# Attention outputs made in columns by pairs of heads, four expert tiles loaded beside the weight ring, and one wait placed later

## The reference, cut to what matters

```python
# part A, layer l
p = sink_softmax(concat([s_loc, s_ctx]), sink)          # 8 heads of 64, 2 key heads
o = p @ v                                               # per head: [128 queries, 64]
o_x = concat([o, local_mixers(...)]) @ w_out[l]
x = layer_norm(ALPHA * x + g1 * o_x, ln1_g[l], ln1_b[l])
y = hier_moe(x * (1 + sc2) + sh2, ...)                  # 2 of 32 experts a token: silu(xb@w1)*(xb@w3) @ w2
# part B, layer l
swa = softmax_with_sink(q_a k_a^T, band) @ v_a          # times a silu gate g_a
fox = softmax(q_b k_b^T + c_i - c_j, causal) @ v_b      # times a silu gate g_b
x += concat([swa, fox, ssm]) @ w_out_2
x += memory_attention(x)
```

## Time and profile before

| what | value |
|---|---|
| median of 3 runs | 2305.1 us (2302.08 to 2305.42) |
| the profiled execution's own time | 2304.22 us |
| its span, first to last instruction | 2302.4 us |
| PE busy | 2035.6 us, 88% of the span |
| mean granted TensorE clock | 0.985 |
| moved by the transfer engines | 640.95 MB, 278 GB/s on average |

### The profile page before, as it was taken

How to read it: one execution, slowest core, us unless ns; L and a number is a source line. 1 busy time by engine, 2 the same in 40 slices (tenths; PEclk the granted TensorE clock), 3 DMA queues, 4 the chain that set the end, 5 groups by cost and what they waited for, 6 DMA issues and landing times.

```text
span 2302.4 us, 30476 instructions
## 1 busy us (share of the span) xinstructions
PE 2035.6 (88%) x11971; PEld 1212.3 (53%) x11972; DVE 786.6 (34%) x1836; ACT 457.2 (20%) x1059; POOL 189.7 (8%) x240
## 2 busy tenths in 40 slices
PE   6999999799877789999877777798999999999998
PEld 4566566444433335757433333344875575775574
DVE  1355674111111116656111111114466312456413
ACT  2142112111111112411111111111123212123112
POOL 1000001111111110001111111111000000000000
PEclk9999999999999999999999999999999999999999
DMA  9235649999999985686999999996343332343230
GB/s 376 110 129 240 255 156 378 423 426 427 427 425 426 425 345 211 236 317 257 424 425 425 424 425 425 427 420 242 134 182 129 111 147 110 147 165 129 95 142 19
DMA packets 62872, 640.95 MB, mean 278 GB/s; under 512 B 15868, under 2 KB 16420, under 8 KB 24240
## 3 DMA queue, kind: packets, MB, share of 16 engines
q1 hardware_dynamic: 41728, 588.39, 61.9%
q0 software_dynamic: 19984, 44.74, 5.5%
q10 hardware_dynamic: 1056, 6.37, 0.7%
HBM read 622.50 MB, written 44.17 MB: 290 GB/s over the span
## 4 chain that ended last, share of the span: by engine, by line
PE 62%; DMA 31%; DVE 4%; ACT 2%; issue 1%; SPq 0%; POOL 0%; DVEq 0%
DMA ring<-in_moe 26%; PE ps L866 10%; PE ps L1037 10%; PE ps L519 8%; PE ps L1051 6%; PE ps L1148 5%; PE ps L507 3%; PE ps L695 3%; DMA ring<-in_denseA 3%; PE ps L1220 2%; PE ps L872 2%; PE ps L1016 2%; PE ps L541 2%; PE ps L771 2%; PE ps L584 1%; DMA ring<-in_denseB 1%
## 5 line engine op out<-in xcount | busy, mean ns | idle before, releaser
L866 PE MATMUL ps<-ring,scr 128*64 128x256 f32 (+1 forms) x4800 | 667.5, 430 | 178.2 <-DMA ring<-in_moe 169.3
L866 PEld LDWEIGHTS ps<-ring,scr 128*64 128x64 f32 x4800 | 333.4, 138 | 485.9 <-DMA ring<-in_moe 239.3
L1833 DVE TENSOR_TENSOR scr<-ps,scr 128x512 f32<-128x512 f32 (+3 forms) x98 | 54.6, 558 | 574.6 <-PE ps L866 487.0
L1037 PE MATMUL ps<-ring,hT 128*128 128x512 f32 (+1 forms) x576 | 245.5, 578 | 5.1 <-ACT hT L1546 5.1
L519 PE MATMUL ps<-ring,hT 128*128 128x512 f32 (+1 forms) x512 | 199.3, 547 | 0.5 <-ACT hT L1516 0.5
L1444 POOL DMA_INDIRECT ys_scratch<-scr,ytab x128 | 125.0, 976 | 825.4 <-DVE scr L2495 791.6
L1670 ACT ACTIVATE scr<-ps 128x512 f32<-128x512 f32 x64 | 38.2, 597 | 760.8 <-PE ps L866 694.0
L2495 DVE COPY scr<-ps 128x1024 f32<-128x1024 f32 x64 | 78.4, 1224 | 269.3 <-PE ps L866 243.4
L1037 PEld LDWEIGHTS ps<-ring,hT 128*128 128x128 f32 x576 | 108.1, 193 | 117.8 <-issue 108.2
L1516 ACT ACTIVATE scr<-ps 128x256 f32<-128x256 f32 (+2 forms) x168 | 71.3, 436 | 403.7 <-PE ps L507 403.7
L519 PEld LDWEIGHTS ps<-ring,hT 128*128 128x128 f32 x512 | 97.3, 193 | 93.0 <-issue 89.2
(11 more groups left out here) (330 smaller groups left out, 2019.2 us busy)
## 6 DMA issues: line engine op xcount, KB each, us to landing
ring<-in_moe SPq DMA_DIRECT2D x192, 2048.0 KB, 15.9
ring<-in_denseB SPq DMA_DIRECT2D x48, 2048.0 KB, 7.7
ring<-in_denseA SPq DMA_DIRECT2D x36, 2048.0 KB, 16.2
scr<-ys_scratch POOLq DMA_DIRECT2D x6, 1024.0 KB, 7.2
modB<-mod_scratch POOLq DMA_DIRECT2D x10, 512.0 KB, 11.3
ring<-kv_scratch SPq DMA_DIRECT2D x2, 2048.0 KB, 8.6
tok_scratch<-hb POOLq DMA_DIRECT2D x6, 512.0 KB, 2.9
memT_scratch<-modB ACTq DMA_DIRECT2D x2, 1024.0 KB, 6.7
```

The lines of the kernel that those rows point to most:

```text
L866: last = mm(out, lhs(c)[:, 0:64], w(c)[:, half * q:half * (q + 1)], start=(c == 0), stop=(c == n - 1))
L1037: last = mm(T["open"][:, 0:cols], hT16[:, c, t * P:(t + 1) * P], w[:, c, 0:cols], start=(c == 0), stop=(c == DC - 1))
L1833: return V.tensor_tensor(out, a, b, op)
```

## The change

- **Attentions in pairs** (the 48 units of part A and 64 of part B; the memory attention keeps its way). The values become the standing operand (64 columns) and the turned weights move (128 columns). The two heads of a pair go to the two column halves of the array, and the result comes out with its columns on the partitions, as `w_out` needs it, so that turning the outputs goes. The weights are now divided by their sum before they are turned, by the DVE (`scaled`), and the PE waits for that (`p_scaled`) and no longer for the exponential. The sink is an extra column of the scores, which takes away the ACT detour. DVE and ACT now go through a pair in the order scores, scores, scale, scale, extras; ACT's side jobs (`serve`) come after both copies of a pair. Some side jobs move one unit later. The gates `ga` and `gb` are made in columns.
- **Tiles beside the ring** (`ASIDE`). Expert tile 3 of layer 0 and expert tiles 3, 7 and 10 of layer 1 get homes of their own in `modB`, `hb`, `S`, `hT` and `scr`, and their transfers are issued before tile 2 of the layer (that of layer 1's tile 3 even before tile 0). The gathers have two buffers in `hb` in place of four for it.
- **The wait on `kv_out`** moves from the end of part A behind the first products of row block 1 in part B.

```diff
+ASIDE = ((3,), (3, 7, 10))
...
-TURNED = ("x0", "x1", "x2", "qb", "kb")
+TURNED = ("x0", "x1", "x2", "qb", "kb", "ga", "gb")
...
+    low_mod, low_rows = (v[:, 2:4, :].rearrange("p a b -> p (a b)") for v in (modB, hb))
+    aside = (((low_mod, low_rows),),
+             ((S[:, 2:4, :].rearrange("p a b -> p (a b)"), low_rows), (low_mod, hT[:, half_tile:2 * half_tile]),
+              (scr[:, 10400:10400 + half_tile], scr[:, 10400 + half_tile:10400 + 2 * half_tile])))
...
+    def in_ring(l, at):
+        return baseM[l] + at - sum(a < at for a in ASIDE[l])
...
+        def paired_attention(units, score, values, nkc, fill):
+            T["p"] += len(units)
+            for i in range(2):
                 score(*units[i])
-            T["bank"] = None
-            def turn_weights(i):
+            fill(0)
+            for i in range(0, len(units), 2):
+                n, h = units[i]
+                for k in (i, i + 1):
+                    need("scaled", p_scaled)
+                    turn_weights(k, nkc(n))
+                    turned = T["tp"]
+                    if k == i:
+                        for at in range(i + 2, min(i + 4, len(units))):
+                            score(*units[at])
+                    if k > 0:
+                        fill(k)
+                if h == 0:
+                    T["bank"] = av_bank()
+                pe.wait_ge(tp_free, turned)
+                for b in range(nkc(n)):
+                    for q in range(2):
+                        last = mm(T["bank"][HD * q:HD * q + HD, h // 2 * P:(h // 2 + 1) * P], values(n, h + q, b),
+                                  sbuf_pT[:, q, b, :], start=(b == 0), stop=(b == nkc(n) - 1))
+                if h == NH - 2:
+                    last.then_inc(av_full, 1)
...
-            attention([(n, h) for n in range(nt) for h in range(NH)],
+            paired_attention([(n, h) for n in range(nt) for h in range(NH)],
                       gqa_score(qTA, kTA, lambda n: 0 if n < NX else 256, lambda n: 512),
                       lambda n, h, k: vA[:, k + (0 if n < NX else 2), (h // GQA) * HD:(h // GQA + 1) * HD],
-                      lambda n: 4 if n < NX else 2, HD, fill)
-            for t in range(nt):
-                need("h", h_ready)
-                turn([hb[:, t, i * P:(i + 1) * P] for i in range(4)])
+                      lambda n: 4 if n < NX else 2, fill)
+            need("h", h_ready, nt)
...
-                    of_rows(mk_at - 2 + j, t, 0, 512)
+                    w = tile(mk_at - 2 + j)
+                    rows_times(lambda c: hb[:, t, c * P:(c + 1) * P] if c < 4 else hT8[:, c, t * P:(t + 1) * P],
+                               lambda c: w[:, c, :], 512)
...
+            def moe_tile(i, at, width):
+                if type(i) is int and at in ASIDE[l]:
+                    n = ASIDE[l].index(at)
+                    pe.wait_ge(aside_in[l][n], 32)
+                    per = half_tile // width
+                    return lambda c: aside[l][n][c // per][:, c % per * width:(c % per + 1) * width]
...
-            for t in range(NX):
-                need("h", h_ready)
-                for c in (0, 4):
-                    turn([mixB[:, t, (c + i) * P:(c + i + 1) * P] for i in range(4)])
+            need("h", h_ready)
+            out_attended(0, 0)
+            need("h", h_ready)
             pe.wait_ge(tp_free, T["tp"])
-            out_attended(0, 0)
...
-            dense(lambda i: d["moe"][l][tile_of(*in_order[i])], 3 * UNROLL - 1, G0)
-            with sp_.Fori(0, E // UNROLL - 1) as i:
+            B0 = blocks_before[l]
+            def load_aside(n):
+                src = d["moe"][l][tile_of(*in_order[ASIDE[l][n]])]
+                for k in range(2):
+                    sp_.dma_start(aside[l][n][k], src[:, k * half_tile:(k + 1) * half_tile]).then_inc(aside_in[l][n], 16)
+            def expert_tile(at):
+                dense(lambda i: d["moe"][l][tile_of(*in_order[at])], 1, in_ring(l, at))
+            if l > 0:
+                sp_.wait_ge(*free_when["turned", l])
+                load_aside(0)
+            expert_tile(0)
+            expert_tile(1)
+            sp_.wait_ge(*free_when["routed", l])
+            sp_.wait_ge(rows_out, (96, 144)[l])
+            if l == 0:
+                sp_.wait_ge(tok_out, 16 * 4)
+                load_aside(0)
+            else:
+                load_aside(1)
+                load_aside(2)
+            for at in range(2, 6 * UNROLL - 1):
+                if at not in ASIDE[l]:
+                    expert_tile(at)
+            with sp_.Fori(1, E // UNROLL - 1) as i:
...
-                if k >= 4:
-                    pool.wait_ge(rows_T, 2 * (K0 + k - 3))
-                pool.indirect_dma_start(hb[:, k % 4, :], None, tok_d,
+                if k >= 2:
+                    pool.wait_ge(rows_T, 2 * (K0 + k - 1))
+                pool.indirect_dma_start(hb[:, k % 2, :], None, tok_d,
...
+        def weights(i, n, h, nk):
+            T["nm"] += 1
+            act.wait_ge(nm_ready, T["nm"])
+            A(sbuf_p[:, i % 2, 0:nk], sbuf_s[:, i % 2, 0:nk], ACT.Exp, bias=nm[:, n, h:h + 1],
+              accum_out=rsum[:, n, h:h + 1]).then_inc(p_ready, 1)
+        def paired_attention(units, nkc, sink, serve, after=None):
+            for i in range(0, len(units), 2):
+                for k in (i, i + 1):
+                    n, h = units[k]
+                    weights(k, n, h, P * nkc(n) + sink)
+                for k in (i, i + 1):
+                    copy_turned(sbuf_pT[:, k % 2, 0:nkc(units[k][0]), :], nkc(units[k][0]))
+                    if after:
+                        after(k)
+                if i > 0:
+                    serve(i - 1)
+                serve(i)
+            serve(len(units) - 1)
...
+        def paired_attention(units, keys, masks, cq, sink, finish, extra, ck=None):
+            def scores(i):
+                n, h = units[i]
+                bank = score_bank()
                 nk = keys(n)
                 s = sbuf_s[:, i % 2, 0:nk]
-                m = masks(n) if masks else None
-                if scale:
-                    tell(ts(s, bank[:, 0:nk], scale(n), None, ALU.mult), sc_free)
-                elif m is None:
+                m = masks(n)
+                if sink:
+                    go(V.tensor_copy(sbuf_s[:, i % 2, nk:nk + 1], snk[:, h:h + 1]))
+                if m is None:
...
+            def scaled(i):
+                n, h = units[i]
+                p = sbuf_p[:, i % 2, 0:keys(n)]
+                dve.wait_ge(p_ready, T["p"] + i + 1)
+                step(V.reciprocal(rinv[:, n, h:h + 1], rsum[:, n, h:h + 1]))
+                tell(ts(p, p, rinv[:, n, h:h + 1], None, ALU.mult), p_scaled)
+            for i in range(0, len(units), 2):
+                for k in (i, i + 1):
+                    scores(k)
+                for k in (i, i + 1):
+                    scaled(k)
+                if i > 0:
+                    extra(i - 1)
+                extra(i)
+                if i > 0 and units[i][1] == 0:
+                    finish(units[i][0] - 1, av_job())
+            extra(len(units) - 1)
+            finish(units[-1][0], av_job())
+            T["p"] += len(units)
...
-                if i == 2:
+                if i == 3:
                     answer()
                     gate_moments((0, 1))
                     root()
-                if i == 4:
+                if i == 5:
                     answer()
                     gate_norm()
...
+            def put_turned(n, bank):
+                tell(V.tensor_copy(hb[:, n, 0:512], bank), av_free)
                 tell(V.tensor_copy(mx[:, 1:2], mx[:, 0:1]), h_ready)
...
-                dve.wait_ge(kv_out, 16 * 2 * DEPTH)
...
                 bank = acc_job()
+                if l == 0 and t == 1:
+                    dve.wait_ge(kv_out, 16 * 2 * DEPTH)
...
-                if i == 12:
+                if i == 13:
```

More of the change, by code:

```diff
@@ new lines, in memory_attention @@
+        def memory_attention(units, score, values, beside):
+            for i in range(2):
+                score(*units[i])
+            for i, (n, h) in enumerate(units):
+                need("p", p_ready)
+                turn_weights(i, 2)
+                turned = T["tp"]
+                if i + 2 < len(units):
+                    score(*units[i + 2])
+                beside(i)
+                pe.wait_ge(tp_free, turned)
+                if h % 2 == 0:
+                    T["bank"] = av_bank()
+                for k in range(2):
+                    last = mm(T["bank"][:, h % 2 * 256:(h % 2 + 1) * 256], sbuf_pT[:, i % 2, k, :], values(h, k),
+                              start=(k == 0), stop=(k == 1))
+                if h % 2 == 1:
+                    last.then_inc(av_full, 1)
@@ L1932, in attention @@
[L1932 to L1939 removed]
+                done()
+                least(n, h, s, sink)
+            def scaled(i):
[4 more added lines that the diff above has]
```

(1 more changed line is left out.)

289 lines of the change are left out of this document (124 added, 165 removed).

## The result

The changed kernel took 2316.8 us (median of 5, 2311.75 to 2318.3) where the kernel before took 2305.1 (median of 5, 2302.08 to 2306.91). The ratio is 1.0048, 95% interval 1.0036 to 1.0061: slower by 0.5%. The forecast was 2280, in a range of 2260 to 2297. The profiled execution took 2318.3, 14.1 more than that of before. Its span is 2316.5 against 2302.4, and the trace splits this difference.

A forecast was written before the change was run, and what follows sets the result against it. It took transfers to bound the expert stretches and TensorE part B's attentions, with part A's mixed. Terms 4.0 - 2.5 + 12 + 0 + 5.1 + 6.0 = 24.6 us gave 2280 us, range 2260 to 2297.

The forecast's parts named there:

- Layer 0's one tile: Layer 0's experts: tile loaded beside the ring, worth at most 4.93 us, against later gathers; taken as 0 (-6 to +3).
- Part B: Both attentions and the unturned outputs in part B: +3.0 us gained per layer (1 to 6), 6.0 for both.
- The sums: Part B's sliding window attention: running sums go out one unit later, back near when needed; priced at 0.8 us a layer.
- The weighing: Multiplying weights with values in two column halves: two records cost what one did, saving 3.0 us per part B attention.
- The forgetting attention: Part B, each layer: VectorE's longer pairs cost 4.9 us against 3.0 saved by weighing; -1.9 us.
- The turns of the outputs: Part B, each layer: attention outputs no longer need turning on TensorE; +3.1 us gained.
- Layer 1's attention: Part A, layer 1: 3.8 us saved before the projection tile's release, less waits and late rows; -2.5 us (-5 to +3).
- Layer 0's attention: Part A, layer 0: 7.6 us saved less 3.6 for first pair, gelu and extras; gain 4 us (1 to 8).
- Layer 1's tiles: Layer 1's experts: three tiles loaded beside the ring into idle transfer time; gain 12 us (8 to 14.8).
- The wait on `kv_out`: Start of part B: the moved wait removes TensorE's idle time; gain 5.1 us (0 to 5.5).
- rival C: Attentions: halves don't overlap or each shape change costs, all weighing savings go; 2304 or 2315 us, chance 0.05.
- Rival B: Layer 0's gathers make TensorE 6 to 8 us late, layer 1's attention gives back 5; 2292 us, chance 0.17.

The follow-up runs named there:

- e6: Changed kernel with layer 0's tile back in the ring, four gather buffers there, and the running sums at unit 12: 2289.72 us, ratio 0.9922 to the kernel before.
- e3: Changed kernel with the running sums turned and stored at unit 12 of the sliding window attention instead of unit 13: 2303.8 us, ratio 0.9995 to the kernel before.
- e13: e6 without dividing the weights by their sums (no reciprocal, no scaling on VectorE): 2663.24 us, a total of no use; only attention stretches are read.
- the twins: Kernel before with six products added ahead of each of 40 part B half products: every other one with 64 standing columns, 2440.1 us; all with 128, 2402.1 us.

## Why the prediction was wrong

The forecast was 24.6 us faster by its own sum, and the trace has 14.1 us slower. With the gathers and the sums mended, e6 gains 18.0, so these two steps are most of the error. By its steps:

- **Layer 0's one tile**, "I take 0 (-6 to +3)": measured -14.1. This is the largest error. The mechanism was named, a gather's whole flight between two turns. The flights were taken from the earlier trace rows, at 13 to 20 us, and the wait was guessed at 3 to 5. But those flights belong to a schedule in which blocks 4 and 5 had gone at 355 and 361. The change put them, two loads and the stores into the same ten microseconds, and the flight became 27.3. The step that failed is that a duration was carried over to a load that it was not measured under.
- **Part B**, "6.0 for both": measured -9.2. Three terms. The sums were priced at 0.8 a layer. The step in which they are awaited lost 5.8 and 4.8, where in e3 it gains 0.8 and 0.9, so they cost 6.7 and 5.6: the slack behind them was nearly nothing, no row of the prediction measured it, and the clock added to the damage. The weighing, priced at 3.0 an attention, brought some 0.3 (four pairs at -0.12, four at +0.2), since the changes of shape took the rest. The forgetting attention was forecast at -1.9, which was -4.9 for VectorE and +3.0 for the weighing; it is -3.0 and -3.1, and by e13 this is all VectorE's, with nothing from the weighing. The stretch at the lower clock lies ahead of its first mark and has no part in it. The turns of the outputs came as forecast, +3.1 against 3.3.
- **Layer 1's attention**, "-2.5 (-5 to +3)": -4.8 up to the last row and -8.2 up to the keys' store. The single waits were right (1.1, 1.3, 1.6 and 1.4 forecast; 1.12, 1.49, 1.36 and 1.29 in the trace). The saving was not 3.8 but some 2.8, at 0.7 for each of four pairs, and what a late normalization does to the clock of the routing was not in the sum.
- **Layer 0's attention**, "Gain 4": -0.4 in this trace, -1.2 to +1.4 in the seven with pairs in part A. Eight weighings at 0.7 are 5.7 us and not 7.6; the five waits for the scaling come to 4.9, where 3.6 was taken; and behind the gelu's wait (2.37 us against 2.0) stands a stretch at the lower clock.
```profile
135.04 0.80 PE L524 MATMUL ps<-cst,scr 128*128 128x128 f32 x4 [2.37 <-DVE scr L1905]
```
- **Layer 1's tiles**, 12: 11.7 between the marks, right there, though 7.6 in the medians of the runs that isolate them with the wait. **The wait on `kv_out`**, 5.1: 6.1 between the marks and 4.6 alone (2.5 to 6.9), right in size; the clock that it gives back was not in the sum.

The rule of the Trainium skill that the prediction weighed ("TensorEngine Tiling (Array Packing)", Key Properties: a change of tiling mode drains TensorE) speaks of such a price, and the runs agree: 0.14 to 0.16 us a change in the twins. The row without idle time, by which the prediction set it aside, could not have shown it: such a price sits in the distance between two starts. At 0.16 and two changes a pair it was rival C's price in kind, though not a loss of all weighing savings, for the halves do overlap. That C's 2315 lies close to the measured 2316.8 is luck: most of the loss is the gathers and the sums, which C does not have. Rival B had the right place, and half of the size. None of the rivals put the gathers, the sums and the shapes together.

What the prediction left out altogether is the clock. Behind idle times of 15.42, 5.14, 2.75 and 2.37 us the trace shows the lower level, and the profiled clock is 0.976 against 0.985. The length of one wait doesn't tell it: the clock falls behind 1.52 us at 1056.21 in the kernel before, and not behind 1.49 at 958.86 in the changed one. The wait for the sums cost 3.7 us more of idle time and some 2 more through the clock.

## What to carry to other kernels

When a change takes buffers from a chain of small transfers, ask what else will be in the same queue when they are issued late, and don't take their flight from the schedule of before. A result that comes back just in time has no slack to spend: find the arrival and the moment of need before moving its start by one place. Count the changes of array shape, and judge a narrower product by the starts of its neighbours, not by its own rows or by idle time.

## What the runs showed of the hardware that was not expected

- A change between 128 and 64 standing columns costs 0.14 to 0.16 us, with no idle time in any row (38.0 us over 240 changes).
- Two column halves given alternately take 1.09 us for 16 records of 128 columns, and 1.58 one after the other; for 8 records it is 0.66 either way.
- Stores issued by GpSimd behind four gathers and two loads, beside a full tile stream, are 27 to 30 us in flight; without the two loads 17 to 19.
- TensorE's clock fell to the lower level behind a wait of 5.14 us (2.4 us lost in the next half product alone), and not behind one of 1.41 us at the same place.
